# Prompt attention with the branch factors applied after the value products: rows of factors through DRAM, plain transposes, GpSimd adding the branches

## The chip, the cores and the metric

The kernel runs on one core of one Trainium2 chip. The metric is the device time of one execution in microseconds (us), lower is better. TensorE (PE), VectorE (DVE), ScalarE (ACT), GpSimd (POOL) and SyncE (SP, which here only issues DMAs) run side by side and meet at semaphores; each engine takes its own instructions in order.

## What is computed

One step of a decoder layer: half-step FFN, a mixer (sparse attention and a pooling mixer), a second FFN, a final norm. The change touches only the attention of the prompt (1024 tokens, 8 query heads of width 64 in 2 KV groups of 4). Each head has three branches over different keys, and their results are added with a gate:

```python
def masked_softmax(s, mask):
    s = jnp.where(mask, s, NEG_INF)
    m = jnp.max(s, axis=-1, keepdims=True)
    e = jnp.where(mask, jnp.exp(s - m), 0.0)
    return e / jnp.maximum(jnp.sum(e, axis=-1, keepdims=True), 1e-30)
...
    o = gates[..., 0:1] * o_c + gates[..., 1:2] * o_s + gates[..., 2:3] * o_w
```

With 16 selected blocks of 64 for 1024 prompt tokens, the selected branch is causal attention over all keys. For a query token and head the result is therefore the sum over the branches of a factor, gate / sum(e), times sum over the keys of e * v. The factor belongs to the query; it can be multiplied in before or after the product with v.

## The kernel before

The kernel is a row of stages with a barrier between them: compression of the cache, FFN 1, input projection, pooling, compression of the prompt, **prompt attention** (stage_attend_prompt, about 1618 to 2098 us), sample attention, output projection, FFN 2, finish.

Prompt attention runs a loop over the two KV groups g. In it, 128 query tokens at a time make a block qt = 0 to 7, and one more iteration, qt = 8, drains. Iteration qt has four **rows** r, one for each head: the scores of block qt and head r (selected keys into slc_bank, window keys and compressed blocks into win_bank; L1895 to L1932), maxima on VectorE (L1853 to L1859), exponentials with their sums on ScalarE (L1757 to L1765) into probs. Between them each row carries a quarter of the **value units** of the block before, qt - 1: one unit is 128 keys of one branch (64 for the compressed one), so block qt - 1 has qt selected units, up to five of the window and one compressed, 3 in the first block and 14 in the last; 74 for each g. For each unit

- TensorE **turns** the probabilities of the four heads (L1884): a matmul with probs as weights and a diagonal matrix that holds the factor of each token, so the factor is multiplied in while the tile is transposed;
- ScalarE takes the high half (L1733) and VectorE the low half (L1798) out of the turn bank, of which there are two;
- TensorE multiplies both halves by the values (L1948, L1949). The product of a unit is issued after the turn of the next one. All branches of a block are summed in one PSUM bank, out_bank[qt % 2].

In row 2 the query tile of the next block is turned first (L1890, a plain transpose of at_dup against the identity). The order is by hand: in each row TensorE issues selected scores, window scores, then its turns and products; VectorE the maxima, then the low halves; ScalarE the first high half, the selected exponential, the second high half, the window exponentials, the rest.

The factors come from VectorE (factors, L1813 to L1821), for heads 0 and 1 at the end of row 2 and for heads 2 and 3 at the end of row 3; GpSimd spreads each pair to diagonals (L1700), and the first turn of the next iteration waits for the second pair (L1882, wait on diag_ready). When a block is summed, ScalarE copies its upper half (L1738, the values' low halves) and VectorE adds it to the lower half in four pieces into mixT (take, L1830), in row 1 of the next iteration but one. SyncE issues nothing in this stage.

## Time and profile before

| what | us |
|---|---|
| median of 3 runs | 3283.76 (3279.31 to 3285.95) |
| the profiled execution | 3281.28 |
| its span | 3279.6 |
| prompt attention, within the span | about 480 |
| PE busy in the whole span | 2924.5 (89%) |
| DVE, ACT, POOL busy in the whole span | 1448.3, 905.5, 311.1 |

### The profile page before, as it was taken

The numbers are of one execution on the slowest core, as the hardware profiler recorded it, in microseconds if no ns is written. First come the engines' busy times: TensorE is split into PE (matmuls) and PEld (weight loads), VectorE is DVE, ScalarE is ACT, GpSimd is POOL, SyncE is SP. The second block draws the span as 40 slices with busy tenths as digits, with TensorE's granted clock in tenths as the row PEclk, the third lists the DMA queues.
The fourth block names the chain that finished last, engine by engine and source line by source line (L and its number), as shares of the span: only waits on it lengthen the run. The fifth ranks groups of instructions, "written<-read, shape, count | busy, mean of one in ns | idle before, by whom it ended". The sixth has DMA issues, their size and how long they took to land. (4 is left out here: it accounts for less than half of the span.)

```text
span 3279.6 us, 48743 instructions
## 1 busy us (share of the span) xinstructions
PE 2924.5 (89%) x18374; PEld 2688.3 (82%) x18374; DVE 1448.3 (44%) x2808; ACT 905.5 (28%) x1537; POOL 311.1 (9%) x294
## 2 busy tenths in 40 slices
PE   4999989999999997885789789687799999999997
PEld 4889879999999996884667667433589999999996
DVE  4444455544444445013255456312326454444445
ACT  4665651111111102111245345233222111111112
POOL 3444410000000001000011011211000000000000
PEclk9999999999999998997579879888899999999999
DMA  4212133211111102102100000365322111111101
GB/s 158 110 56 110 62 105 105 64 38 38 40 50 42 47 0 87 33 26 77 35 1 1 2 1 1 125 183 158 112 58 62 42 53 49 38 38 51 38 13 53
DMA packets 168574, 193.84 MB, mean 59 GB/s; under 512 B 11431, under 2 KB 154536, under 8 KB 165679
## 3 DMA queue, kind: packets, MB, share of 16 engines
q1 hardware_dynamic: 161623, 141.58, 14.2%
q0 software_dynamic: 6816, 50.49, 4.2%
q8 instruction: 81, 1.33, 0.2%
q14 instruction: 54, 0.44, 0.0%
HBM read 178.30 MB, written 17.91 MB: 60 GB/s over the span
## 5 line engine op out<-in xcount | busy, mean ns | idle before, releaser
L407 ACT ACTIVATE f_act_gate<-f_act_gate 128x352 f32<-128x352 f32 x132 | 65.8, 498 | 1186.2 <-DVE f_act_gate L464 1186.1
L501 DVE SCALAR_TENSOR_TENSOR trunk<-f_down,trunk 128x352 f32<-128x352 f32 x528 | 275.8, 524 | 207.8 <-PE f_down L104 207.8
L102 PE MATMUL f_up<-f_h_hi,f_gu_hi 128*128 128x352 f32 x1056 | 344.6, 326 | 0.0
L102 PE MATMUL f_gate<-f_h_hi,f_gu_hi 128*128 128x352 f32 x1056 | 344.3, 326 | 0.0
L104 PE MATMUL f_up<-f_h_hi,f_gu_lo 128*128 128x352 f32 x1056 | 342.8, 325 | 0.0
L104 PE MATMUL f_gate<-f_h_hi,f_gu_lo 128*128 128x352 f32 x1056 | 342.5, 324 | 0.0
L102 PE MATMUL f_down<-f_a_hi,f_wd_hi 128*128 128x352 f32 x1056 | 340.6, 323 | 0.0
L103 PE MATMUL f_gate<-f_h_lo,f_gu_hi 128*128 128x352 f32 x1056 | 340.5, 322 | 0.0
L103 PE MATMUL f_up<-f_h_lo,f_gu_hi 128*128 128x352 f32 x1056 | 340.1, 322 | 0.0
L103 PE MATMUL f_down<-f_a_lo,f_wd_hi 128*128 128x352 f32 x1056 | 338.5, 321 | 0.0
L104 PE MATMUL f_down<-f_a_hi,f_wd_lo 128*128 128x352 f32 x1056 | 338.1, 320 | 0.0
L102 PE MATMUL cs_sum<-cs_x_hi,cs_w_hi 128*128 128x256 f32 (+1 forms) x768 | 229.9, 299 | 32.6 <-DVE cs_x_lo L1152 21.4
L104 PE MATMUL cs_sum<-cs_x_hi,cs_w_lo 128*128 128x256 f32 (+1 forms) x768 | 217.5, 283 | 0.0
L103 PE MATMUL cs_sum<-cs_x_lo,cs_w_hi 128*128 128x256 f32 (+1 forms) x768 | 217.4, 283 | 0.0
L102 PEld LDWEIGHTS f_gate<-f_h_hi,f_gu_hi 128*128 128x128 f32 x1056 | 199.6, 189 | 1.3 <-DVE f_gu_lo L447 1.1
L102 PEld LDWEIGHTS f_up<-f_h_hi,f_gu_hi 128*128 128x128 f32 x1056 | 199.9, 189 | 0.0
L1884 PE MATMUL at_turn_bank<-at_diag,at_probs 128*128 128x128 f32 (+1 forms) x1184 | 177.7, 298 | 24.6 <-POOL at_diag L1700 20.3
L1884 PEld LDWEIGHTS at_turn_bank<-at_diag,at_probs 128*128 128x128 f32 (+1 forms) x1184 | 162.4, 203 | 45.3 <-issue 39.6
L103 PEld LDWEIGHTS f_gate<-f_h_lo,f_gu_hi 128*128 128x128 f32 x1056 | 198.8, 188 | 0.2
L103 PEld LDWEIGHTS f_up<-f_h_lo,f_gu_hi 128*128 128x128 f32 x1056 | 198.9, 188 | 0.0
L103 PEld LDWEIGHTS f_down<-f_a_lo,f_wd_hi 128*128 128x128 f32 x1056 | 198.4, 188 | 0.0
L102 PEld LDWEIGHTS f_down<-f_a_hi,f_wd_hi 128*128 128x128 f32 x1056 | 198.1, 188 | 0.0
(333 smaller groups left out, 5812.3 us busy)
## 6 DMA issues: line engine op xcount, KB each, us to landing
as_pages<-in_cache_kv_slc_dram SPq DMA_DIRECT2D x192, 128.0 KB, 2.3
f_gu_raw<-in_w_ffn_gate_dram SPq DMA_DIRECT2D x44, 512.0 KB, 4.5
f_gu_raw<-in_w_ffn_up_dram SPq DMA_DIRECT2D x44, 512.0 KB, 5.7
f_wd_raw<-in_w_ffn_down_dram SPq DMA_DIRECT2D x22, 1024.0 KB, 5.0
as_pages<-in_cache_kv_slc_dram POOLq DMA_DIRECT2D x64, 128.0 KB, 3.2
in_w_raw<-in_w_in_dram SPq DMA_DIRECT2D x4, 1304.0 KB, 5.9
x_saved<-trunk SPq DMA_DIRECT2D x1, 4224.0 KB, 16.2
trunk<-x_saved SPq DMA_DIRECT2D x1, 4224.0 KB
```

The source lines that it names most:

```text
L102: pe.matmul(out, w_hi, x_hi, start=first, stop=False)
L103: pe.matmul(out, w_hi, x_lo, start=False, stop=False)
L104: return pe.matmul(out, w_lo, x_hi, start=False, stop=last)
L407: act.activation(act_gate[:, b, :], act_gate[:, b, :], ACT.Silu).then_inc(silu_done, 1)
L501: dve.scalar_tensor_tensor(xT[:, m, chunk(c)], down_bank[n % 4][:, 0:CH], 0.5, xT[:, m, chunk(c)], ALU.mult, ALU.add).then_inc(down_free, 1)
L1884: tr = pe.matmul(bank[0:rows, h * P:(h + 1) * P], probs[qt % 2][:, h, lo:lo + rows], diag[:, qt % 2, h, branch, :], start=True, stop=True)
```

## The change

- The turn of a value unit is a transpose against the identity (L1909 of the new kernel) of the unscaled exponentials; it waits for the exponentials of all four heads instead of the diagonals. The diagonals and their GpSimd work are gone.
- Each of the three branches of a block is summed alone. The branches (selected, window, compressed) take the two out banks in turn. VectorE multiplies each closed sum by rows of factors (scale, L1858), 128 x 512 from PSUM and SBUF to SBUF, right after the low half of the unit that follows the branch's last; the compressed branch's comes behind the first unit of the next block.
- The factors of all four heads are made at once, at the end of row 0 of the next iteration (L1841 to L1849). SyncE writes them to DRAM transposed, 128 x 12 single floats, waits for that to land, and reads the 12 x 128 rows back into every partition (spread). Every scale of that block waits for spread.
- GpSimd adds the three scaled branches, copies the upper half and adds the halves (gather, four kinds of step), two iterations later, between its query copies; after the last iteration of g for the last two blocks. ScalarE's copy and VectorE's take are gone. GpSimd's program is no longer a loop over g, and it copies the first two key tiles of g = 1 ahead of the last two gathers of g = 0.

The core of the diff:

```diff
+    BRANCHES = (SLC, WIN, CMP)
+    ends = [[max(u for u, unit in enumerate(value_units(qt)) if unit[0] == branch) for branch in BRANCHES]
+            for qt in range(QT)]
+    behind = {}
+    for x, n in products.items():
+        _, qt, u = x
+        if u in ends[qt] and n + 1 < PRODUCTS:
+            follower = [y for y in products if products[y] == n + 1][0]
+            behind[follower] = (qt, ends[qt].index(u), BRANCHES[ends[qt].index(u)])
...
-        diag = mem.sb(scope, "at_diag", [P, 2, GROUP, 3, P])
+        spread = mem.sb(scope, "at_spread", [P, 3 * GROUP, P])
+        scaled = [mem.sb(scope, f"at_scaled{i}", [P, 3, GROUP, P]) for i in range(2)]
...
+            @block.sync
+            def _(sp):
+                for g in range(N_KV):
+                    for qt in range(QT):
+                        n = QT * g + qt
+                        sp.wait_ge(factor_ready, n + 1)
+                        if n >= 2:
+                            sp.wait_ge(spread_landed, 16 * (n - 1))
+                        sp.dma_start(factor_rows[qt % 2].rearrange("k p -> p k"),
+                                     factor[:, qt % 2].rearrange("p r b -> p (r b)"),
+                                     allow_slow_non_contiguous=True).then_inc(rows_saved, 16)
+                        sp.wait_ge(rows_saved, 16 * (n + 1))
+                        if n >= 1:
+                            sp.wait_ge(scaled_done, 3 * n + RING)
+                        sp.dma_start(spread[:], factor_rows[qt % 2].unsqueeze(0).to_broadcast([P, 3 * GROUP, P])
+                                     ).then_inc(spread_landed, 16)
...
+                def gather(g, qt):
+                    n, m = QT * g + qt, scaled[qt % 2]
+                    pool.wait_ge(scaled_done, 3 * n + 2 + RING)
+                    pool.tensor_tensor(m[:, 0], m[:, 0], m[:, 1], ALU.add).then_inc(added, 1)
+                    pool.wait_ge(scaled_done, 3 * n + 3 + RING)
+                    pool.wait_ge(added, 4 * n + 1)
+                    pool.tensor_tensor(m[:, 0], m[:, 0], m[:, 2], ALU.add).then_inc(added, 1)
+                    pool.wait_ge(added, 4 * n + 2)
+                    pool.tensor_copy(upper[:], m[HD:2 * HD, 0]).then_inc(added, 1)
+                    pool.wait_ge(added, 4 * n + 3)
+                    for half, sem in enumerate((added, out_taken)):
+                        pool.tensor_tensor(mixT[half * HD:(half + 1) * HD, 2 * g:2 * g + 2, qt * P:(qt + 1) * P],
+                                           m[0:HD, 0, half::2, :], upper[:, half::2, :], ALU.add).then_inc(sem, 1)
+                        if half == 0:
+                            pool.wait_ge(added, 4 * n + 4)
+                    pool.wait_ge(out_taken, n + 1 + RING)
...
+                        if qt >= 2:
+                            gather(g, qt - 2)
+                    if g + 1 < N_KV:
+                        for x in LEAD[:2]:
+                            duplicate(g + 1, x)
+                    for qt in range(QT - 2, QT):
+                        gather(g, qt)
...
-                                take_upper(g, qt - 2)
...
+                def factors(g, qt):
                     for i in range(2):
-                        dve.wait_ge(exped[i], HEADS * g + GROUP * qt + PAIR * (pair + 1) + ONE)
-                    if qt >= 2:
-                        dve.wait_ge(diag_ready, 2 * QT * g + 2 * (qt - 2) + pair + 1 + ONE)
-                    else:
-                        dve.wait_ge(diag_ready, 2 * QT * g + ONE)
-                    heads = slice(PAIR * pair, PAIR * pair + PAIR)
-                    f = factor[:, qt % 2, heads, :]
-                    s0 = STEPS * g + (4 * qt + 2 * pair + 2 if qt else 3 * pair)
-                    dve.tensor_scalar(f, sums[:, qt % 2, heads, :], 1e-30, None, ALU.max).then_inc(dve_step, 1)
+                        dve.wait_ge(exped[i], HEADS * g + GROUP * (qt + 1) + ONE)
+                    f = factor[:, qt % 2]
+                    s0 = STEPS * g + (2 * qt + 1 if qt else 0)
...
+                def scale(g, qt, n, branch):
+                    dve.wait_ge(pv_done, PRODUCTS * g + products[("v", qt, ends[qt][n])] + 1 + RING)
+                    dve.wait_ge(spread_landed, 16 * (QT * g + qt + 1))
+                    dve.wait_ge(out_taken, QT * g + qt - 1 + RING)
+                    rows = spread[:].rearrange("p (r b) n -> p b r n", b=3)[:, branch]
+                    dve.tensor_tensor(scaled[qt % 2][:, n], out_bank[(3 * qt + n) % 2][:].rearrange("p (r n) -> p r n", r=GROUP),
+                                      rows, ALU.mult).then_inc(scaled_done, 1)
...
+                                    if x[0] == "v" and x in behind:
+                                        scale(g, *behind[x])
+                            if qt > 0 and r == 0:
+                                factors(g, qt - 1)
+                    scale(g, QT - 1, 2, CMP)
...
-                            pe.wait_ge(diag_ready, 2 * QT * g + 2 * (qt + 1) + ONE)
+                        pe.wait_ge(exped[0 if branch == SLC else 1], HEADS * g + GROUP * (qt + 1) + ONE)
                         pe.nop(nofuse=True)
                         for h in range(GROUP):
-                            tr = pe.matmul(bank[0:rows, h * P:(h + 1) * P], probs[qt % 2][:, h, lo:lo + rows],
-                                           diag[:, qt % 2, h, branch, :], start=True, stop=True)
+                            tr = pe.transpose(bank[0:rows, h * P:(h + 1) * P], probs[qt % 2][:, h, lo:lo + rows],
+                                              K["ident"][:])
...
+                    n = BRANCHES.index(branch)
+                    first, last = u == (ends[qt][n - 1] + 1 if n else 0), u == ends[qt][n]
+                    bank = out_bank[(3 * qt + n) % 2]
                     pe.wait_ge(split, TURNS * g + at[x] + 1 + RING)
                     if v == 0:
                         pe.wait_ge(v_ready, g + 1)
-                    if u == 0:
-                        pe.wait_ge(out_taken, QT * g + max(0, qt - 1) + ONE)
+                    if first:
+                        pe.wait_ge(scaled_done, 3 * (QT * g + qt) + n + 1)
                     pe.nop(nofuse=True)
                     values = (vc_split[0:rows] if source is None else v_split[:, source[0], source[1]]
                               ).rearrange("p c d -> p (c d)")
-                    last = u == len(value_units(qt)) - 1
-                    pe.matmul(out_bank[qt % 2][:], values, turned_hi[v % 2][0:rows, :], start=(u == 0), stop=False)
-                    pe.matmul(out_bank[qt % 2][:], values, turned_lo[v % 2][0:rows, :], start=False,
+                    pe.matmul(bank[:], values, turned_hi[v % 2][0:rows, :], start=first, stop=False)
+                    pe.matmul(bank[:], values, turned_lo[v % 2][0:rows, :], start=False,
                               stop=last).then_inc(pv_done, 1)
-                    if last:
-                        pe.wait_ge(pv_done, PRODUCTS * g + v + 1 + RING)
-                        pe.nop().then_inc(out_done, 1)
```

TensorE at the end of row 2 of iteration 1, and behind the line of dots its row 3 (the scores between are left out). Before:

```order
L1876 REGISTER_ALU
L1884 MATMUL at_turn_bank_290<-at_diag,at_probs_277 128x128 x4
L1941 REGISTER_ALU
L1943 ISA
L1948 MATMUL at_out_bank_292<-at_turned_hi_283,at_v_split 128x512
L1949 MATMUL at_out_bank_292<-at_turned_lo_285,at_v_split 128x512
...
L1884 MATMUL at_turn_bank_291<-at_diag,at_probs_277 64x128 x4
L1939 REGISTER_ALU
L1948 MATMUL at_out_bank_292<-at_turned_hi_284,at_v_split 128x512
```

The same place after:

```order
L1902 REGISTER_ALU
L1909 MATMUL at_turn_bank_292<-ident,at_probs_277 128x128 x4
L1969 REGISTER_ALU
L1971 ISA
L1975 MATMUL at_out_bank_294<-at_turned_hi_285,at_v_split 128x512
L1976 MATMUL at_out_bank_294<-at_turned_lo_287,at_v_split 128x512
...
L1909 MATMUL at_turn_bank_293<-ident,at_probs_277 64x128 x4
L1967 REGISTER_ALU
L1971 REGISTER_ALU
L1975 MATMUL at_out_bank_295<-at_turned_hi_286,at_v_split 128x512
```

The instructions stand in the same places; the turn reads the identity, and the next branch's product goes to the other bank (295).

VectorE from the window maxima of row 0 of iteration 3 on. Before, the row's low half, then in row 1 the take of block 1:

```order
L1857 TENSOR_REDUCE at_neg_max<-at_win_bank 128x1
L1859 TENSOR_REDUCE at_neg_max<-at_win_bank 128x1
L1787 REGISTER_ALU
L1798 TENSOR_TENSOR at_turned_lo_285<-at_turn_bank_290,at_turned_hi_283 128x512
L1826 REGISTER_ALU
L1830 ISA
L1830 TENSOR_TENSOR trunk<-at_out_bank_293,at_upper 64x128
```

After, behind the same low half, the scale of block 1's compressed branch and the factors of block 2:

```order
L1881 TENSOR_REDUCE at_neg_max<-at_win_bank 128x1
L1883 TENSOR_REDUCE at_neg_max<-at_win_bank 128x1
L1820 REGISTER_ALU
L1831 TENSOR_TENSOR at_turned_lo_287<-at_turn_bank_292,at_turned_hi_285 128x512
L1854 REGISTER_ALU
L1858 TENSOR_TENSOR at_scaled_281<-at_out_bank_295,at_spread 128x512
L1841 TENSOR_SCALAR at_factor<-at_sums 128x12
...
L1843 RECIPROCAL at_factor<-at_factor 128x12
...
L1849 TENSOR_TENSOR at_factor<-at_factor,z 128x12
```

In row 2 of that iteration the first scale with these factors (block 2, selected branch) stands between two low halves:

```order
L1826 SCALAR_TENSOR_TENSOR at_q_split<-at_turn_bank_293,at_q_split 64x512
L1820 REGISTER_ALU
L1831 TENSOR_TENSOR at_turned_lo_288<-at_turn_bank_292,at_turned_hi_286 128x512
L1854 REGISTER_ALU
L1855 ISA
L1858 TENSOR_TENSOR at_scaled_280<-at_out_bank_294,at_spread 128x512
L1820 REGISTER_ALU
L1831 TENSOR_TENSOR at_turned_lo_287<-at_turn_bank_293,at_turned_hi_285 128x512
```

What moved on VectorE: the factors came from the ends of rows 2 and 3 to the end of row 0 of the next iteration, and the take became three scales.

## Rows read from the trace of the kernel before

**Rows 1.** Stretches of prompt attention: us, busy (x instructions) by engine, granted clock, DMA share.
```profile
1640.00:1656.00 16.00, 12.50 (x57) 11.16 (x58) 7.03 (x23) 6.95 (x29) 3.49 (x3) 0.52 0.00 1
...
1750.00:1775.00 25.00, 22.84 (x154) 18.44 (x153) 15.46 (x32) 12.08 (x29) 3.49 (x3) 1.00 0.00 1
...
sum 481.00, PE 398.98 PEld 321.53 DVE 250.63 ACT 220.94 POOL 60.87; mean PE 24.94 PEld 20.10 DVE 15.66 ACT 13.81 POOL 3.80
```

**Rows 2.** Groups of prompt attention: busy, mean ns of one, then idle before.
```profile
L1884 PE MATMUL at_turn_bank<-at_diag,at_probs 128*128 128x128 f32 (+1 forms) x1184 | 177.7, 298 | 24.6 <-POOL at_diag L1700 20.3 <-PE at_out_bank L1949 2.1 <-DVE at_turned_lo L1798 1.0
...
L1700 POOL TENSOR_TENSOR at_diag<-ident,at_factor 128x768 f32<-128x768 f32 x32 | 47.0, 1469 | 346.5 <-DVE at_factor L1821 346.5
...
L1830 DVE TENSOR_TENSOR trunk<-at_out_bank,at_upper 64x128 f32 x64 | 18.1, 283 | 15.0 <-ACT at_upper L1738 14.1
...
L1815 DVE RECIPROCAL at_factor<-at_factor 128x6 f32<-128x6 f32 x32 | 6.1, 191 | 1.1
```

**Rows 3.** Waits of prompt attention: us in total, times, longest.
```profile
PE at_turn_bank L1884 <- POOL at_diag L1700: 20.3, 14, 3.1
...
DVE trunk L1830 <- ACT at_upper L1738: 14.1, 10, 1.7
```

**Rows 4.** One row without a query turn (qt 6, r 1): start, duration, instruction.
```profile
1773.85 0.99 PEld L1884 LDWEIGHTS at_turn_bank<-at_diag,at_probs 128*128 128x128 f32 x8
...
1775.14 0.60 ACT L1733 ACTIVATE at_turned_hi<-at_turn_bank 128x512 fp32r<-128x512 f32 x1 [2.50 <-PE at_turn_bank L1884]
...
1775.63 1.00 ACT L1757 ACTIVATE at_probs<-at_slc_bank,at_neg_max 128x896 f32<-128x896 f32 x1
...
1777.25 0.69 DVE L1798 TENSOR_TENSOR at_turned_lo<-at_turn_bank,at_turned_hi 128x512 fp32r<-128x512 f32 x1 [0.71 <-ACT at_turned_hi L1733]
...
1778.39 0.19 PEld L1895 LDWEIGHTS at_slc_bank<-at_kT_hi,at_q_split 128*128 128x128 f32 x1
```

**Rows 5.** The next row, with a query turn (r 2), timeline.
```profile
1780.60 0.43 PEld L1890 LDWEIGHTS at_turn_bank<-ident,at_dup 128*128 128x128 f32 x4
...
1780.99 0.97 PEld L1884 LDWEIGHTS at_turn_bank<-at_diag,at_probs 128*128 128x128 f32 x8
...
1781.30 0.60 ACT L1728 ACTIVATE at_q_split<-at_turn_bank 128x512 fp32r<-128x512 f32 x1 [2.31 <-PE at_turn_bank L1890]
```

**Rows 6.** VectorE's low halves that frame the later scale, timeline, two iterations.
```profile
1688.30 0.69 DVE L1798 TENSOR_TENSOR at_turned_lo<-at_turn_bank,at_turned_hi 128x512 fp32r<-128x512 f32 x1 [2.85 <-ACT at_turned_hi L1733]
...
1700.03 0.69 DVE L1798 TENSOR_TENSOR at_turned_lo<-at_turn_bank,at_turned_hi 128x512 fp32r<-128x512 f32 x1 [0.46 <-ACT at_turned_hi L1733]
...
1772.05 0.69 DVE L1798 TENSOR_TENSOR at_turned_lo<-at_turn_bank,at_turned_hi 128x512 fp32r<-128x512 f32 x1 [0.86 <-ACT at_turned_hi L1733]
...
1783.40 0.69 DVE L1798 TENSOR_TENSOR at_turned_lo<-at_turn_bank,at_turned_hi 128x512 fp32r<-128x512 f32 x1 [0.78 <-ACT at_turned_hi L1733]
```

**Rows 7.** VectorE's low halves in the last block's drain, timeline.
```profile
2076.72 0.69 DVE L1798 TENSOR_TENSOR at_turned_lo<-at_turn_bank,at_turned_hi 128x512 fp32r<-128x512 f32 x1 [1.35 <-ACT at_turned_hi L1733]
...
2086.36 0.69 DVE L1798 TENSOR_TENSOR at_turned_lo<-at_turn_bank,at_turned_hi 128x512 fp32r<-128x512 f32 x1 [0.67 <-ACT at_turned_hi L1733]
...
2089.54 0.69 DVE L1798 TENSOR_TENSOR at_turned_lo<-at_turn_bank,at_turned_hi 128x512 fp32r<-128x512 f32 x1 [0.67 <-ACT at_turned_hi L1733]
```

**Rows 8.** DMA issues: KB each, median us to landing.
```profile
as_pages<-in_cache_kv_slc_dram SPq DMA_DIRECT2D x192, 128.0 KB, 2.3
...
f_gu_raw<-in_w_ffn_gate_dram SPq DMA_DIRECT2D x44, 512.0 KB, 4.5
...
as_kc<-kc_saved SPq DMA_DIRECT2D x1, 1024.0 KB, 4.9
```

**Rows 9.** GpSimd's groups in the whole kernel: a two-operand step of nearly 512 columns.
```profile
L1009 POOL TENSOR_TENSOR cs_x_lo<-cs_x,cs_x_hi 128x516 fp32r<-128x516 f32 x128 | 170.1, 1329 | 231.2 <-ACT cs_x_hi L1066 231.2
```

**Rows 10.** The last stage, where TensorE only transposes: instructions of fin_bank, granted clock.
```profile
3271.00:3272.00 1.00, 1.00 (x7) 1.00 (x6) 0.61 (x2) 0.50 0.00 0
...
3274.00:3275.00 1.00, 1.00 (x12) 0.92 (x10) 1.00 (x3) 1.00 0.70 283
```

More of the change, by code:

```diff
@@ L1599, in stage_attend_prompt @@
     HEADS = QT * GROUP
-    PAIR = 2
     def win_tiles(qt):
@@ L1675, in _ @@
             @block.gpsimd
             def _(pool):
-                pool.sem_inc(diag_ready, ONE)
                 def duplicate(g, x):
                     m = dups[x]
-                    before = TURNS * g + ONE
-                    if m >= 2:
-                        before += at[[y for y in dups if dups[y] == m - 2][0]] + 1
+                    before = ONE
+                    if DUPS * g + m >= 2:
+                        earlier = [y for y in dups if dups[y] == (m - 2) % DUPS][0]
+                        before += TURNS * ((DUPS * g + m - 2) // DUPS) + at[earlier] + 1
@@ L1705, in _ @@
-                with pool.Fori(0, N_KV) as g:
-                    for x in LEAD:
-                        duplicate(g, x)
+                def gather(g, qt):
[14 more added lines that the diff above has]
+                    pool.wait_ge(out_taken, n + 1 + RING)
@@ L1708, in _ @@
+                for x in LEAD:
+                    duplicate(0, x)
+                for g in range(N_KV):
+                    if g > 0:
+                        for x in LEAD[2:]:
+                            duplicate(g, x)
                     for qt in range(QT):
@@ L1710, in _ @@
                             duplicate(g, ("q", qt + 1))
-                        for pair in range(2):
-                            diagonals(g, qt, pair)
+                        if qt >= 2:
[5 more added lines that the diff above has]
+                        gather(g, qt)
             @block.scalar
@@ L1820, in factors @@
                         dve.wait_ge(dve_step, s0 + 3)
-                    dve.tensor_tensor(f, f, z[:, qt, bass.ds(OFF_GATE + g * 3 * GROUP + 3 * PAIR * pair, 3 * PAIR)]
+                    dve.tensor_tensor(f, f, z[:, qt, bass.ds(OFF_GATE + g * 3 * GROUP, 3 * GROUP)]
                                       .rearrange("p (r b) -> p r b", b=3), ALU.mult).then_inc(factor_ready, 1)
-                def take(g, t):
-                    dve.wait_ge(upper_done, QT * g + t + 1)
-                    for r in range(GROUP):
-                        half = slice((r % 2) * HD, (r % 2 + 1) * HD)
-                        cols = slice(r * P, (r + 1) * P)
-                        last = dve.tensor_tensor(mixT[half, bass.ds(2 * g + r // 2, 1), t * P:(t + 1) * P],
-                                                 out_bank[t % 2][0:HD, cols].unsqueeze(1), upper[:, cols].unsqueeze(1),
-                                                 ALU.add)
-                    last.then_inc(out_taken, 1)
+                def scale(g, qt, n, branch):
[5 more added lines that the diff above has]
+                                      rows, ALU.mult).then_inc(scaled_done, 1)
                 with dve.Fori(0, N_KV) as g:
@@ L1845, in _ @@
                         for r in range(GROUP):
-                            if r == 1 and qt >= 2:
-                                take(g, qt - 2)
                             n = GROUP * qt + r
@@ L1862, in _ @@
                                     low(g, x)
-                            if qt < QT and r >= 2:
-                                factors(g, qt, r - 2)
-                    take(g, QT - 1)
+                                    if x[0] == "v" and x in behind:
[3 more added lines that the diff above has]
+                    scale(g, QT - 1, 2, CMP)
             @block.tensor
```

46 lines of the change are left out of this document (16 added, 30 removed).

## The prediction

> **What bounds the kernel now.** I read the stretches first, since the change touches one stage only. Prompt attention is 481 us of the span, and TensorE is busy in 399 of them, VectorE in 251, ScalarE in 221, GpSimd in 61 [rows 1]. In the middle of the stage TensorE works 22.8 of 25 us at the full granted clock; at the start of a group it works 12.5 of 16 at a clock of 0.52 [rows 1]. The costliest group is the turn, 1184 matmuls or eight for each of 148 units, 177.7 us busy [rows 2]. Then the waits: TensorE waited 20.3 us for the diagonals, in 14 of 16 blocks, and VectorE 14.1 us for ScalarE's copy of the upper half [rows 3].
>
> A busy TensorE isn't yet the bound, so I followed one row in order of time [rows 4]. The row starts its first turn at 1773.85; the first high half starts at 1775.14, the selected exponential behind it at 1775.63, the second low half at 1777.25, and the next row's scores at 1778.39. The scores of a head wait for the exponentials of the head before and stand behind the second product, so a row is a ring: scores, first turn, ScalarE's first high half and exponential, second high half, second low half, product, scores. The first turn is on the ring; the second and third are beside ScalarE's work. The reader is to see this, since it decides what a cheaper turn is worth: once a row, not three times.
>
> **The turn, removed and added.** The turn of a unit with diagonals takes 1.29 us from its first weight load to ScalarE's start (1773.85 to 1775.14) [rows 4]. The query tile is already a plain transpose of the same four 128 x 128 tiles, four records instead of eight: 0.70 us (1780.60 to 1781.30), and TensorE goes on after 0.39 us (1780.99) [rows 5]. So a plain turn on the ring saves 0.59 us. Rows of r = 2 start with the query turn, which doesn't change; their ring passes through it, and I give them nothing. That leaves rows 1 and 3 of iteration 1, rows 0, 1, 3 of iterations 2 to 6 and four rows of iteration 7: 21 for each g, 42 x 0.59 = 25 us. Were TensorE the bound throughout, it would be 148 x (0.99 - 0.39) = 89 us; were the low halves the bound, nothing. I take 25, since the ring is what the rows show.
>
> In the drain there are no scores. Two turn banks make two units a round: low halves at 2086.36 and 2089.54, 3.18 us for two units [rows 7], with one turn on the round. 14 rounds in the two groups, each 0.59 us shorter: 8 us. The most it could be is TensorE's own work, 2 x 0.60 a round, 17 us; the least nothing.
>
> **The wait for the diagonals** goes: 20.3 us, all of it ahead of the first turn, on the ring [rows 3]. What is late next there is the exponentials of the fourth head, for which the scores wait anyway. GpSimd's 32 diagonals, 1.47 us each, go with it [rows 2].
>
> **VectorE's own work.** Removed for each block: four adds of 0.28 us [rows 2], about 0.9 us of waiting (14.1 / 16) [rows 3] and one of two sets of factors. Added: three scales, 128 x 512 from PSUM, which I price as the low half of that shape, 0.69 us [rows 4]: 2.1 us against some 2.0 and the factors. I put them at nothing together; VectorE is busy in half the stage, and ScalarE loses its copy, which was beside the ring. Were none covered, 48 x 0.69 = 33 us would be lost, less 32 regained; so 0 with a bound of 10 either way. Two out banks now turn over three times a block: a product that opens a branch waits for the scale two branches back, which is a whole row old except where that scale itself is late.
>
> **The factors' way through DRAM** is the added wait, and it decides the case. SyncE has nothing else in its queue. The chain: factors done, write of 1536 single floats, its landing, read of 128 x 6 KB = 768 KB, its landing, then the scale of the selected branch. Queued behind that scale on VectorE are all later low halves and maxima, so TensorE and ScalarE stop soon after.
>
> How much room there is, from the low halves that stand there now. In iteration 6 the last low half of row 0 ends at 1772.74 and the first unit's of row 2 at 1784.09 [rows 6], 11.35 us apart; the factors take 0.75 of it (three small steps, the reciprocal 0.19 us [rows 2], with a semaphore between them; an estimate from that row), and the row between shortens by 0.59: 10.0 us of room. In iteration 3 it is 1688.99 to 1700.72 [rows 6], 11.7 us, but the take (1.1), the compressed scale (0.7), the factors (0.75) and the turns of two rows come off: 8.5. In the drain the low half of the third unit ends at 2077.41, that of the ninth at 2087.05 [rows 7], 9.6 us; six units at 0.3 less each and the factors off: 6.9. I take 8.5 for iterations 1 to 4, 10 for 5 to 7 and 6.9 for the drain.
>
> How long the way is. No row shows a write of single floats. The nearest is the load of 1024 pieces of 512 bytes: 4.5 us, against 2.3 for 128 pieces of 1 KB, so 2.2 us for about 900 more pieces [rows 8]; 1536 pieces make 2.3 + 3.5 = 5.8 us. From below it is 2.3 us, as a small DMA; from above I take twice the time of a piece, since a piece smaller than anything in the trace may need its surroundings read and written: 2.3 + 7 = 9.3. The read lies between 512 KB in 4.5 and 1024 KB in 4.9 us [rows 8], fewer and larger pieces: 4.2. From below 3.6, half way from the small load to the large one; from above 6, a quarter over the 1024 KB, since all partitions read the same 6 KB and no row does that. With 0.3 for the semaphores the way takes 10.3 us, between 6.2 and 15.6. Per group the stall is 4 x 1.8 + 3 x 0.3 + 3.4 = 11.5, or **23 us** in all; at 6.2 none; at 15.6 it is 4 x 7.1 + 3 x 5.6 + 8.7 = 53.9, or 108 us. I take 23, by the row of small pieces.
>
> The Trainium skill speaks against this write: DMA: Bandwidth & Descriptors, Rules for kernel authors, has a strided last dimension lower to one descriptor for each element, and its section Bandwidth measured about 10.5 ns a packet, which with its fixed 2.0 us would make the write an estimated 3.0 us. The sum would then lose its stalls almost whole and end near 3237. No trace here shows it.
>
> **The tail.** The stage now ends after scale 0.69, GpSimd's second add, copy, and two half adds. A GpSimd add of two operands over 516 columns takes 1.33 us [rows 9]: 0.69 + 1.33 + 0.66 + 1.33 = 4.0 us, against copy 0.60 and 4 x 0.28 = 1.7. Plus 2.3 us, once; in g = 0 it lies beside the engines' own turn of the loop. In the iterations the gather, 5.3 us, has a whole iteration of over 15 us.
>
> **The clock.** TensorE gets less to do, and at the start of each group it runs at 0.52 while busy 78% [rows 1]. I allow 5 us for a rise that comes later. The row that bears on it: in the last stage TensorE does nothing but transposes, and its clock stands at 0.50 at 3271 and at 1.00 at 3274 [rows 10]. TensorE: Matmul & The Clock Gate of the Trainium skill, Part 4: PE-mode transpose, says that transposes don't count as busy for the clock in the same way; the trace disagrees, and by it I don't lower the clock of the whole stage.
>
> **The sum.** 25 + 8 + 20.3 = 53 off; 23 + 2.3 + 5 = 30 on; net 23 off the profiled 3281.3: 3258. The median stands 2.5 above that execution, so **3261**.
>
> **The rivals.** *The way is hidden.* If it lands within 7 us, no block waits, and the time is 3283.8 - 53 + 7 = 3238. For it: the queue is empty and the DMA engines are idle in this stage (share 0.00 [rows 1]). Against it: two landings one after the other, each 2.3 at the very least. *The way is long: slower.* Each further us costs 16, eight blocks in two groups. The gain is used up at 12 us: 2 x (4 x 3.5 + 3 x 2 + 5.1) = 50 against 53 - 7 = 46. At 14 us it is 2 x (4 x 5.5 + 3 x 4 + 7.1) = 82: 3320; at 15.6, 3346. It takes only that a float costs 70 ns more in its queue than I reckon, and nothing in the trace excludes that. *A tie,* where the way takes 11.5 to 12.2 us. *The clock halves.* If transposes don't hold it, the lower level, 1.2 GHz, stays. TensorE took 12.5 / 57 = 0.22 us for each instruction at a clock of 0.52 and 22.8 / 154 = 0.15 at 1.00 [rows 1], 1.48 times. Of its 399 us, 310 are left without the 89; three quarters of them, at full clock now, would grow by 0.48 x 232 = 111 us, nearly all on the ring: 3367. Against it stand the transposes alone, which raised the clock [rows 10].
>
> **How the numbers follow.** Forecast (way 7.5 to 11.5 us) 0.37, 3240 to 3275; hidden 0.2; tie 0.08; long way 0.3; clock 0.05. A measurement of this kernel can tell about 0.2%, 6.6 us. With the edges of the cases, faster than 3277 has 0.58, same 0.1, slower than 3290 0.32. For 8 in 10 the range takes in the hidden way and most of the long one: 3234 to 3338.
>
> **What would show it.** The median from issue to landing of the two new DMAs, 5.8 and 4.2; VectorE's idle time ahead of the scales put down to spread, 23 us in 16; the turn with four records and no wait on GpSimd; rows of r = 1 some 0.6 us shorter and rows of r = 2 not; the drain's rounds 2.6 us. Wrong would be the sum if rows shorten by three turns (then TensorE was the bound), if the write lands in over 8 us, or if the granted clock of the middle of the stage leaves 1.00.

## The result and the profile after

| | us |
|---|---|
| before, median of 4 runs | 3284.57 (3279.31 to 3285.95) |
| after, median of 4 runs | 3326.59 (3323.61 to 3329.84) |
| ratio | 1.0131, 95% interval 1.0114 to 1.0149 |
| predicted | 3261 (3234 to 3338) |

The change costs 42 us. The time lies in the range; the direction was wrong. All of it is in prompt attention, which now ends about 2139 instead of 2098.

Stretches of the kernel after, columns as in [rows 1]:

```profile
1640.00:1656.00 16.00, 12.45 (x63) 10.76 (x63) 6.48 (x19) 6.74 (x27) 0.00 (x0) 0.58 0.04 0
1656.00:1676.00 20.00, 12.11 (x45) 8.13 (x44) 9.22 (x20) 5.95 (x21) 5.21 (x6) 0.60 0.15 40
...
1750.00:1775.00 25.00, 16.67 (x94) 12.53 (x94) 13.43 (x23) 10.13 (x26) 3.96 (x5) 0.86 0.14 33
...
sum 521.00, PE 345.95 PEld 253.73 DVE 262.21 ACT 209.81 POOL 88.23; mean PE 23.06 PEld 16.92 DVE 17.48 ACT 13.99 POOL 5.88
```

TensorE has 53 us less to do than in [rows 1] (345.95 for 398.98) and the stage takes 40 us more. In the middle it works 16.67 of 25 us where it worked 22.84, and the granted clock is 0.86 there instead of 1.00.

Groups, the first two answering to [rows 2], the turn and the scale:

```profile
L1909 PE MATMUL at_turn_bank<-ident,at_probs 128*128 128x128 f32 (+1 forms) x592 | 104.9, 306 | 4.8 <-DVE at_q_split L1826 4.8
...
L1858 DVE TENSOR_TENSOR at_scaled<-at_out_bank,at_spread 128x512 f32<-128x512 f32 x48 | 32.8, 683 | 108.2 <-DMA at_spread<-factor_rows 106.1 <-PE at_out_bank L1976 2.1
```

The eight records of a turn are four, the wait for GpSimd of [rows 3] is gone, and in its place the scales wait 106.1 us for the factor rows. The view of the waits:

```profile
PE at_out_bank L1975 <- DVE at_turned_lo L1831: 116.1, 73, 8.8
DVE at_scaled L1858 <- DMA at_spread<-factor_rows: 106.1, 16, 8.7
```

All 16 blocks wait, 6.6 us each on average, and TensorE's products wait 116.1 us in all for low halves, the longest of them for those that stand behind a waiting scale on VectorE. One block in order of time, SyncE's two issues, then VectorE:

```profile
1785.63 0.37 SPq L1693 DMA_DIRECT2D factor_rows<-at_factor  x1
1797.09 0.32 SPq L1699 DMA_DIRECT2D at_spread<-factor_rows  x1
```

```profile
1785.21 0.39 DVE L1849 TENSOR_TENSOR at_factor<-at_factor,z 128x12 f32<-128x12 f32 x1
...
1794.56 0.69 DVE L1831 TENSOR_TENSOR at_turned_lo<-at_turn_bank,at_turned_hi 128x512 fp32r<-128x512 f32 x1 [0.78 <-ACT at_turned_hi L1773]
1800.91 0.69 DVE L1858 TENSOR_TENSOR at_scaled<-at_out_bank,at_spread 128x512 f32<-128x512 f32 x1 [5.66 <-DMA at_spread<-factor_rows]
```

The write takes 11.46 us from its issue to the read's (1785.63 to 1797.09). The read lands in 4.2, as the view of the DMA issues has it:

```profile
at_spread<-factor_rows SPq DMA_DIRECT2D x16, 768.0 KB, 4.2
```

I had put the write at 5.8 and its upper bound at 9.3. The 16 blocks lie between 9.5 and 12.1, with a mean of 11.1.

### The profile page after: what moved, and what is told of

It reads as the page before. It is cut to its first block and busy times, and to the rows that moved or that the text cites. A ratio compares the mean times of both kernels' runs of the same rounds, so it can differ in the third digit from the quotient of the medians.

```text
span 3321.9 us, 47407 instructions
## 1 busy us (share of the span) xinstructions
PE 2872.5 (86%) x17782; PEld 2619.5 (79%) x17782; DVE 1459.9 (44%) x2742; ACT 894.8 (27%) x1521; POOL 338.8 (10%) x342
## 5 line engine op out<-in xcount | busy, mean ns | idle before, releaser
L104 PEld LDWEIGHTS f_down<-f_a_hi,f_wd_lo 128*128 128x128 f32 x1056 | 197.9, 187 | 0.0
L104 PEld LDWEIGHTS f_gate<-f_h_hi,f_gu_lo 128*128 128x128 f32 x1056 | 197.9, 187 | 0.0
```

The lines of the kernel that those rows point to most:

```text
L104: return pe.matmul(out, w_lo, x_hi, start=False, stop=last)
```

## The experiments

All times are medians; the kernel before stood at 3282.6, 3282.0 and 3280.6 beside the three groups of runs (first the four from no_way to pe_rows, then b_ident, b_no_factors and pe_win, then flat, b_plain and b_fill), so sums across groups are good to about 2 us.

| kernel | us | against before, 95% |
|---|---|---|
| no_way | 3201.4 | 0.9740 to 0.9773 |
| turn_mm | 3239.3 | 0.9847 to 0.9880 |
| half_write | 3300.9 | 1.0044 to 1.0078 |
| pe_rows | 3209.7 | 0.9762 to 0.9794 |
| b_ident | 3240.6 | 0.9856 to 0.9894 |
| b_no_factors | 3238.3 | 0.9851 to 0.9885 |
| pe_win | 3223.0 | 0.9800 to 0.9835 |
| flat | 3202.7 | 0.9754 to 0.9781 |
| b_plain | 3206.3 | 0.9754 to 0.9784 |
| b_fill | 3266.8 | 0.9948 to 0.9974 |

**no_way: what is the way worth?**

```diff
-            @block.sync
-            def _(sp):
...
+                pool.memset(spread[:], 1.0).then_inc(spread_landed, 16)
...
-                    dve.wait_ge(spread_landed, 16 * (QT * g + qt + 1))
+                    dve.wait_ge(spread_landed, 16)
```

> The kernel after without the factors' way: SyncE does nothing, GpSimd sets spread to 1.0 once, no scale waits for a DMA (leaves out the factors, all other work stays). Theory (the wait of 106 us ahead of the scales is the whole loss, and it lies on the ring): that wait gone, 3326.6 - 93 = 3234 (93 is what the rows r = 2 and the two drains are longer for it), near the hidden-way rival of the prediction, 3238; granted clock of the middle of the stage back at 1.00. Rival A (the stall also covered work: three scales a block and GpSimd's adds cost something of their own): 3255 to 3275. Rival B (transposes alone don't hold the clock): 3280 or more, with a clock under 0.9 in the middle of the stage.

3201.4, lower than every case. The way costs 125 us (123 with each kernel set against the kernel before of its own group), not the expected 93, and the rest of the change gains 81, not the prediction's 46. None of the cases on record had these sizes. A table of the rows shows where; each number is the time from one row's selected exponential to the next one's (g = 0):

| iteration | kernel | into row 1 | row 2 | row 3 | next row 0 |
|---|---|---|---|---|---|
| 2 | before | 5.73 | 4.69 | 4.87 | 7.37 |
| 2 | after | 4.77 | 4.69 | 9.88 | 6.54 |
| 2 | no_way | 3.65 | 3.58 | 4.14 | 4.24 |
| 6 | before | 7.36 | 6.17 | 8.33 | 8.16 |
| 6 | after | 6.27 | 6.17 | 15.28 | 6.37 |
| 6 | no_way | 6.27 | 6.17 | 7.82 | 6.36 |

The stall stands in the interval into row 3 (7.5 us in iteration 6). In iteration 2 after is also 1.1 us slower into rows 1 and 2, where nothing waits for a DMA. The stretches show the clock there; after, then no_way:

```profile
1656.00:1660.00 4.00, 0.50 (x3) 0.05 (x1) 0.00 (x0) 0.59 (x1) 0.00 (x0) 1.00 0.34 107
1660.00:1664.00 4.00, 0.45 (x1) 0.47 (x2) 2.21 (x6) 1.15 (x6) 0.00 (x0) 0.51 0.24 94
1664.00:1668.00 4.00, 4.00 (x15) 2.39 (x14) 2.06 (x5) 1.15 (x5) 1.28 (x1) 0.50 0.00 0
1668.00:1672.00 4.00, 3.73 (x16) 2.90 (x15) 3.29 (x8) 1.25 (x7) 2.76 (x4) 0.50 0.13 1
```

```profile
1656.00:1676.00 20.00, 15.15 (x91) 10.05 (x88) 14.96 (x31) 11.30 (x38) 6.50 (x7) 1.00 0.00 0
```

TensorE is nearly idle from 1656 to 1664 in after; the clock goes from 1.00 to 0.50 (1.2 GHz) and stays there while the next rows run. In no_way it has the same kind of work and stays at 1.00. Over the stage, after is 82 us longer than no_way in the intervals into row 3, 21 in the two drains, and 21 in the 48 other intervals, which hold no stall. All of these last 21 lie in iterations 1 to 4; in iterations 5 to 7 the same intervals agree within 0.1 us. So the intervals with the 106 us of stall are 103 longer, and the rows behind them 21. The lower clock is shown beside the latter in iteration 2; that it makes up all 21 is inferred.

**turn_mm: what is the plain turn worth?** On no_way's base:

```diff
-                            tr = pe.transpose(bank[0:rows, h * P:(h + 1) * P], probs[qt % 2][:, h, lo:lo + rows],
-                                              K["ident"][:])
+                            tr = pe.matmul(bank[0:rows, h * P:(h + 1) * P], probs[qt % 2][:, h, lo:lo + rows],
+                                           K["ident"][:], start=True, stop=True)
```

> As no_way, but each turn is an ordinary matmul against the identity, as it was before in form, not a transpose (eight records for four; nothing waits for it more than before). Theory of the prediction (a turn counts once a row, on the ring): 42 x 0.59 in the rows and 14 x 0.59 in the drains, 33 us over no_way. Rival A (TensorE is the bound): 148 x 0.60 = 89 us over no_way. Rival B (the low halves on VectorE are the bound): within 7 us of no_way.

38 us over no_way, beside the expected 33 and far from 89. In iteration 6 the intervals are 7.03, 6.19, 8.32 and 7.08 for no_way's 6.27, 6.17, 7.82 and 6.36: no_way is shorter into rows 1, 3 and 0 and the same into row 2, whose first turn is the query's. Of the 38 us, 32 lie in the rows and 6 in the drains. So a turn counts once a row, as the prediction's ring has it, and not three times.

**half_write: is it the number of floats?**

```diff
-                        sp.dma_start(factor_rows[qt % 2].rearrange("k p -> p k"),
-                                     factor[:, qt % 2].rearrange("p r b -> p (r b)"),
+                        k = 3 * GROUP if n < 2 else 3 * GROUP // 2
+                        sp.dma_start(factor_rows[qt % 2][0:k].rearrange("k p -> p k"),
+                                     factor[:, qt % 2].rearrange("p r b -> p (r b)")[:, 0:k],
```

> The kernel after, but from the third block on only 6 of the 12 factor rows are written (768 single floats for 1536), the read stays whole (leaves out half of the factors). Theory (the write costs by the piece): 2.3 + half of (11.5 - 2.3) = 6.9 us from issue to the read's issue, the way 11.3 instead of 15.8, stalls about 40 us instead of 106, time about 3265. Rival (a fixed price of the transposed form, or the landing of 128 partitions): write stays above 10 us, time within 7 us of 3326.

Missed by both. The writes of six rows took 8.2 to 10.6 us, 9.1 on average, not 6.9 and mostly not above 10; the stalls were 82 us, and the time fell by 26 instead of 60. Half of the pieces save about 2 of 11 us, so most of the write isn't paid by the piece.

**pe_rows: a write of whole rows.** TensorE transposes the 128 x 12 factors in one more step of the turn banks:

```diff
-                        sp.dma_start(factor_rows[qt % 2].rearrange("k p -> p k"),
...
+                        sp.dma_start(factor_rows[qt % 2], rows_sb[:, qt % 2]).then_inc(rows_saved, 16)
...
+                        tr = pe.transpose(bank[0:3 * GROUP, 0:P], factor[:, x[1] % 2].rearrange("p r b -> p (r b)"),
+                                          K["ident"][:])
...
+                        act.activation(rows_sb[:, x[1] % 2], bank[0:3 * GROUP, 0:P], ACT.Copy).then_inc(hi_done, 1)
```

> The kernel after, but TensorE transposes the factors (128 x 12 to 12 x 128, one more step of the turn banks in row 1, ScalarE copies it out), and SyncE writes 12 rows of 512 bytes instead of 1536 single floats; same result. Theory: write 2.3 us, read 4.2, and about 2 us more until the rows stand in SBUF: the way 8.8 us instead of 15.8, stalls under 10 us in all; the extra step costs up to 1 us a block on the ring: 3238 + 6 + 10 = 3254, faster than both kernels. Rival (the read or its landing is what takes the time, not the write): 3300 or more. Rival (the extra step in the ring of turn banks costs as much as it saves): 3280.

3209.7, faster than both kernels. The write of 12 x 512 bytes takes 1.29 us from issue to issue. The extra step costs 1.2 us in the interval into row 2 (iteration 6: 7.38 for 6.17). No scale waits for spread. The expectation was 44 us too high: it started from 3238 without stalls, where no_way measured 3201.

**b_ident and b_no_factors: where do the other 43 us come from?** On the kernel before:

```diff
-                            diagonals(g, qt, pair)
...
-                            pe.wait_ge(diag_ready, 2 * QT * g + 2 * (qt + 1) + ONE)
+                        pe.wait_ge(exped[0 if branch == SLC else 1], HEADS * g + GROUP * (qt + 1) + ONE)
...
-                                           diag[:, qt % 2, h, branch, :], start=True, stop=True)
+                                           K["ident"][:], start=True, stop=True)
```

b_no_factors also drops the call of factors in rows 2 and 3.

> The kernel before with the turn's matmul against the identity (eight records a turn as before), waiting for the exponentials; the diagonals and their GpSimd work are gone, the factors are still made on VectorE at the ends of rows 2 and 3, the take stays (leaves out the multiplication by the factors). It removes the wait for the diagonals alone. Theory (that wait is worth what the waits say, 20.3 us, as the prediction had it): 3283 - 20 = 3263. Rival A (it is worth all that turn_mm gained over the kernel before, 43 us): 3240. Rival B (the exponentials are late next): over 3275.

> As b_ident, and VectorE makes no factors in the rows at all (leaves out the factors). Theory (the factors at the end of row 3 wait for ScalarE's last exponentials and stand ahead of the next row's maxima; the rows r = 3 are 19 us shorter in turn_mm than in the kernel before, which the prediction put at nothing): 20 us below b_ident, 3243. Rival (the rest of the gain is in the take and ScalarE's copy, or in GpSimd's order between the groups): within 6 us of b_ident.

b_ident came out at 3240.6: taking out a wait of 20.3 us [rows 3] was worth 41. Between the two profiled executions, 19 us lie in the intervals into row 0, 13 in the other rows and 11 in the drains. The theory that the wait is worth its length falls. b_no_factors lies within b_ident's runs, so the factors on VectorE cost nothing there. I had read the shorter intervals into row 0 as the factors' place; they were the diagonals. What doubled the wait shows in the kernel before at the turn from iteration 3 to 4:

```profile
1700.00:1704.00 4.00, 3.98 (x29) 3.13 (x27) 2.92 (x7) 1.56 (x5) 0.94 (x1) 1.00 0.03 6
...
1708.00:1712.00 4.00, 2.87 (x16) 2.32 (x15) 1.55 (x3) 0.56 (x2) 2.02 (x2) 0.76 0.00 0
1712.00:1716.00 4.00, 3.61 (x14) 2.87 (x13) 1.03 (x2) 1.79 (x5) 0.00 (x0) 0.50 0.00 0
1716.00:1720.00 4.00, 4.00 (x29) 3.54 (x28) 2.82 (x7) 2.02 (x7) 0.00 (x0) 0.89 0.00 0
```

Behind the wait the clock is at 0.50, and 14 matmuls are done from 1712 to 1716 for 29 in each of the slices 1700 and 1716. The front's stretches of 16 to 25 us average this away. Iteration 4's first row, which runs there, takes 7.82 us into row 1, for b_ident's 6.31. To test the clock:

**b_fill: the wait kept, but filled.** On the kernel before, whole:

```diff
                         if u == 0:
+                            pe.nop(nofuse=True)
+                            for h in range(5):
+                                pe.matmul(bank[:, (h % 4) * P:(h % 4 + 1) * P], K["ident"][:], K["ident"][:],
+                                          start=True, stop=True)
                             pe.wait_ge(diag_ready, 2 * QT * g + 2 * (qt + 1) + ONE)
```

> The kernel before, whole, with five matmuls of the identity (128 x 128 each, some 1.2 us together) issued ahead of the wait for the diagonals in the first turn of each block; their output is overwritten. The wait for the diagonals thereby isn't shorter, TensorE is only busy in it. Theory (b_ident gained 42 us for a wait of 20.3 because TensorE's granted clock falls to its lower level behind the wait and stays there for 4 us and more): the clock no longer falls, and a good part of the other 22 us comes back although work is added: 3262 to 3272. Rival (the 22 us come from the rows' order or from GpSimd, not from the clock): 3282 or more.

3266.8: useless work (the five matmuls took 1.36 us where I looked, at 1704.69) makes the kernel 13.7 us faster. The same stretches of time now, and one in the drain of g = 0:

```profile
1708.00:1712.00 4.00, 3.19 (x21) 2.65 (x22) 1.50 (x3) 2.86 (x8) 0.00 (x0) 1.00 0.00 0
1712.00:1716.00 4.00, 3.40 (x27) 3.06 (x26) 3.64 (x9) 2.48 (x5) 0.00 (x0) 1.00 0.00 0
...
1824.00:1828.00 4.00, 3.70 (x13) 2.91 (x13) 0.69 (x1) 0.97 (x2) 0.00 (x0) 0.50 0.02 4
```

So some 14 of the 21 us beyond the wait are the clock. Most of them came back in rows 1 and 2 of iterations 2 to 4 (iteration 2: 4.15 and 3.57 us, for 5.73 and 4.69 before). In iterations 5 and 6 b_fill's intervals are those of the kernel before within 0.05 us, and there the kernel before keeps its clock behind waits of 1.2 and 1.0 us (1.00 from 1735 to 1747 and from 1764 to 1776). A wait of 1.1 us ahead of iteration 4 had brought it down, so the length of the wait alone doesn't tell. In the drains the clock fell all the same and nothing came back; what the 11 us that b_ident saved there are made of, beyond the wait, stays open.

**b_plain: the sum closed.** b_ident with pe.transpose for pe.matmul in the turn.

> b_ident with plain transposes for the turns: the kernel before, less the diagonals, and with the new turn, but with neither factors' way nor scales nor GpSimd's adds (leaves out the factors). Theory (the turn is worth 38 us here too, as turn_mm against no_way): 3241 - 38 = 3203, so scales, adds and tail cost nothing beside no_way's 3201. Rival (VectorE's scales cost something that other parts of the change give back): 3190.

3206.3: the turn is worth 34 us here. The scales, GpSimd's adds and the tail, which b_plain lacks and no_way has, cost nothing that can be seen; b_plain is even 5 us slower. Two things stand beside that. Its clock was 0.53 in 1656 to 1676 for no_way's 1.00, in g = 0 alone; pe_rows had such a late rise in g = 1 alone (1.00 from 1656 to 1676, but 0.50 from 1858 to 1868), so it can differ between two groups of one execution, and why stays open. And in both groups b_plain is 0.45 to 0.63 us slower into row 1 of iterations 3 to 5, the interval in which its VectorE still has the take.

**write_curve and write_shape: what makes the write dear?** Another size or shape in each block of one kernel, each kernel run once; the first two lines are write_curve's. apart is a DRAM tensor of 128 rows of 1024 bytes, close one of 128 rows of 64 bytes.

```diff
+                            sp.dma_start(out[0:k].rearrange("k p -> p k"), f[:, 0:k],
...
+                            sp.dma_start(out.rearrange("k p -> (k p)").rearrange("(p k) -> p k", k=3 * GROUP),
...
+                            sp.dma_start(apart[:, 0, 0:1], f[:, 0:1],
...
+                            sp.dma_start(close[:, 0:1], f[:, 0:1],
...
+                            sp.dma_start(close.rearrange("p k -> (p k)")[0:P * k].rearrange("(p k) -> p k", k=k), f[:, 0:k],
```

> The kernel after with a write of another size in each block: 12, 12, 8, 6, 4, 3, 2, 1 factor rows for the blocks of g = 0, then for g = 1 all twelve untransposed as 128 pieces of 48 bytes, 12, 10, 6, 4, 2, 1, and 128 pieces again (leaves out or misplaces factors). From SyncE's issue of the write to its issue of the read. Known: 11.5 us for 12 rows, 8.5 for 6, and 1.3 for 12 pieces of 512 bytes. Theory A (a fixed part and a price per piece, 3.9 ns, from the two known sizes): 5.5 + 0.5 per row, so 6.0 us for one row, and the 128 pieces of 48 bytes as one row of 128 singles, 6.0. Theory B (pieces to neighbouring words of DRAM hold each other up, which saturates): one row 3 us or less and a curve that flattens; the 128 pieces of 48 bytes under 3 us.

> The kernel after with a write of another shape in each block of a group: blocks 0 and 1 as it is (1536 single floats); block 2 one factor row, 128 single floats to neighbouring words of DRAM; 3 the same 128 floats, each 1024 bytes from the next; 4 each 64 bytes from the next; 5, 6, 7: 128 pieces of 8, 16 and 32 bytes to neighbouring places (leaves out or misplaces factors). From SyncE's issue of the write to its issue of the read. Theory A (a piece of 4 bytes is dear of itself): 7 us in blocks 2, 3 and 4, and less from 8 bytes on. Theory B (pieces that share a short stretch of DRAM hold each other up): 7 us in block 2, under 2 us in block 3, and growing less with the size of the piece. Theory C (the form of the source, one float from each of 128 partitions, costs it): 7 us in all.

By rows: 12 rows 9.8 to 10.9 us, 6 rows 8.2 and 9.8, 4 rows 8.1 and 10.1, 2 rows 7.9 and 9.4, 1 row 6.9 and 7.3; the whole factors as 128 pieces of 48 bytes 1.41, twice. Theory A had the flat curve and missed the 48 bytes; theory B had the 48 bytes and missed the single row, which it put at 3 us or less. In write_shape, SyncE's issues of write and read, in turn for one row of neighbouring floats, for floats 1024 bytes apart, and for pieces of 8 and of 16 bytes:

```profile
1696.88 0.32 SPq L1699 DMA_DIRECT2D factor_rows<-at_factor  x1
1703.63 0.32 SPq L1714 DMA_DIRECT2D at_spread<-factor_rows  x1
1719.51 0.32 SPq L1702 DMA_DIRECT2D factor_apart<-at_factor  x1
1720.91 0.32 SPq L1714 DMA_DIRECT2D at_spread<-factor_rows  x1
...
1767.72 0.32 SPq L1709 DMA_DIRECT2D factor_close<-at_factor  x1
1770.71 0.32 SPq L1714 DMA_DIRECT2D at_spread<-factor_rows  x1
1794.35 0.32 SPq L1709 DMA_DIRECT2D factor_close<-at_factor  x1
1795.76 0.32 SPq L1714 DMA_DIRECT2D at_spread<-factor_rows  x1
```

6.75, 1.40, 2.99 and 1.41 us; the second group gave 7.53, 2.35, 2.98 and 1.40. Floats 64 bytes apart took 3.16 and 1.41, and pieces of 32 bytes 1.40 twice. Of write_shape's theories B holds: the same 128 floats cost 1.4 to 2.4 us when 1024 bytes apart and about 7 side by side. A piece of 4 bytes isn't dear of itself, and neighbours aren't either from 16 bytes on; dear are pieces of 4 bytes, and less so of 8, side by side. Why, and why 12 rows cost 11 and not 7 us, no run shows. The Trainium skill, DMA: Bandwidth & Descriptors, Specifications, says that below 512 bytes a transfer does a read-modify-write; no run here shows one. Pieces of 48, 32 and 16 bytes landed in 1.4 us all the same, so to be that small isn't enough to make a write dear here.

**flat: the way without a transpose.** The factors are written as they stand, and the scale reads them with a step of 12 floats:

```diff
-                        sp.dma_start(factor_rows[qt % 2].rearrange("k p -> p k"),
+                        sp.dma_start(factor_rows[qt % 2].rearrange("k p -> (k p)").rearrange("(p k) -> p k", k=3 * GROUP),
...
-                    rows = spread[:].rearrange("p (r b) n -> p b r n", b=3)[:, branch]
+                    rows = (spread[:].rearrange("p k n -> p (k n)")
+                            .rearrange("p (n r b) -> p b r n", b=3, r=GROUP)[:, branch])
```

> The kernel after, but nothing is transposed on the way: SyncE writes the factors as they stand, 128 pieces of 48 bytes, reads them back into every partition in that order, and each scale reads spread with a step of 12 floats; same result. Theory (the write costs 1.4 us in this form, as in write_curve; the way is 1.4 + 4.2 = 5.6 us and shorter than the room; nothing is added elsewhere): no_way's 3201, within 4. Rival A (VectorE reads a stride of 48 bytes more slowly, say 1.4 us for 0.68 a scale, 48 of them, partly on the ring): 3215 to 3240. Rival B (the room isn't there while other things are late): 3210 to 3220 with a wait for spread of over 5 us.

3202.7 (3202.1 to 3206.5), 2.3% faster than before and 1.4 us above no_way's median (3.4 with each set against its own kernel before). Its DMA issue of the write, and the group of its scales:

```profile
factor_rows<-at_factor SPq DMA_DIRECT2D x16, 6.0 KB, 1.4
```

```profile
L1858 DVE TENSOR_TENSOR at_scaled<-at_out_bank,at_spread 128x512 f32<-128x512 f32 x48 | 50.6, 1054 | 0.0
```

No scale waits; from issue to issue the writes took 1.40 to 2.57 us. Rival A's premise is true, a scale takes 1.05 us for 0.68, 48 of them 18 us in all; its price isn't: no interval of iteration 6 is over 0.3 us longer than in no_way. So the factors' way costs nearly nothing in this form, and what made the change slow is the form of the write.

**pe_win: pe_rows without the extra step.** The factors are made in the middle of row 0, behind its first low half, and transposed into spare columns of the window bank in row 1.

```diff
+                                    if r == 0 and qt > 0 and x == turns(qt, r)[0]:
+                                        factors(g, qt - 1)
...
+                                        pe.wait_ge(exped[1], HEADS * g + GROUP * qt + r + ONE)
+                                        turn_rows(g, qt - 1)
```

> As pe_rows (12 rows of 512 bytes written), but the extra step isn't in the ring of turn banks: the factors are made behind the first low half of row 0, TensorE transposes them into spare columns of the window bank ahead of row 1's window scores, VectorE copies them out ahead of the window maximum; same result as the reference's. Theory (the extra step costs pe_rows 1.2 us in each row r = 1 of iterations 5 to 7 and a little in the first three iterations of g = 1, and nothing waits for the way): 3210 - 7 = 3203, no_way's 3201 within 3. Rival (VectorE's steps in the middle of row 0 delay the low half and with it the row): 3210 or more.

The rival: 3223.0. Into row 2 of iteration 6 it is 6.17 as in no_way, but into row 1 it is 7.41 for 6.27: the three steps of the factors and their gaps took 1.46 us there (1776.34 to 1777.80), and they stand ahead of a low half; at the row's end, in no_way, they cost nothing seen. The lead isn't the whole of it: in iteration 2 the interval is 6.15 for 3.65, and the two drains, in which two scales waited 6.1 us in all for spread, contrary to the expectation, are 9 us longer.

## Why the prediction was wrong, step by step

Times in us. The terms are measured in different kernels and needn't add up to 42.

| term | predicted | measured | by |
|---|---|---|---|
| plain turns, rows and drains | -33 | -38, -34 | turn_mm, b_plain |
| wait for the diagonals | -20 | -41 | b_ident |
| VectorE's own work | 0 ± 10 | none seen (no_way 5 faster) | b_plain against no_way |
| clock from less work | +5 | none in no_way; a late rise in b_plain and pe_rows | stretches |
| the tail | +2.3 | about +2.8 | from the last low half, after and before |
| the way | +23 | +125 | after against no_way |

- **The step that failed** is the price of the write. I took 5.8 us "by the row of small pieces" and bounded it at 9.3; it took 11.1 on average. The row had 512-byte pieces and says nothing about words that share a stretch of DRAM. The bound was made by doubling the price of a piece, which keeps the wrong form: one row of 128 floats already costs 7 us. Nor did the lower bound hold that each landing takes 2.3 us at the very least: pe_rows' write took 1.29. The text's "70 ns more in its queue" is too much as well: 5.3 us too little over 1536 floats on 16 DMA engines is 55 ns a float on each. And the 3.0 us that it worked out from the Trainium skill, DMA: Bandwidth & Descriptors, Bandwidth, divides 10.5 ns a packet by 16 engines without saying so; one packet behind another it would be 18 us, and the measured 11.1 is neither.
- **The room and the rate were right.** From the end of the factors to the start of the scale the way took 15.6 us on average; less a stall of 6.6 that leaves 9.0 us of room, and the three values taken give 8.9. At 15.6 us the text has 108 us of stall; the trace has 106. The read was put at 4.2, and its median landing is 4.2. That the way met its own upper bound is luck: the write went 1.8 us over its bound of 9.3, and the read, 4.5 us from issue to scale, stayed 1.5 under its bound of 6.
- **The diagonals' wait** was taken at its length. This is the second failed step, in the other direction: it was worth twice that, for two thirds of the surplus because TensorE's clock fell behind it (b_fill). The text weighed the clock for the amount of work and not for the gaps. The same mechanism fits the 21 us that the rows behind the new stalls are longer. TensorE: Matmul & The Clock Gate of the Trainium skill, HAM oscillation, describes waits for a DMA between bursts that bring the lower level back each time; the rows of after agree (1.00 in the slice from 1656, then 0.51 and 0.50 in the next two, while TensorE does almost nothing from 1656 to 1664).
- **The turn** was right in mechanism and close in size: 32 us in the rows for the 25 worked out, 6 in the drains for 8. In the drain a round takes 2.72 us in no_way (low halves at 1801.71 and 1804.43) for 3.18 in [rows 7] and the predicted 2.6.
- **The tail** takes 4.7 us (last scale 2134.32, GpSimd's last add ends 2139.02) for the 4.0 worked out. From the last low half to the end it is 6.4 us after and 3.6 before.
- **The rival that came true** is the long way. It gave 3346 at 15.6 us; the rest of the gain, 81 instead of 46, brought the time down, and the slower rows behind the stalls took 20 of it back. That 3327 lies within the range is luck too: two steps failed in opposite directions, and without the underrated wait the time would have lain above 3338. The rival of the halved clock didn't come: with the same transposes no_way's clock is 1.00 from 1656 to 1676.

## What to carry to other kernels

A transposing write of single floats to DRAM was dear here because neighbouring words were written as pieces of their own: write in the order in which the partitions hold the data, and let the engine that reads it do the stride. A wait of TensorE can cost its length and the lower clock behind it, so read the granted clock in slices of a few us around each wait before pricing it. When a term is bounded from a row of another form, widen the bound by what the form could change and not by a factor on its price.

## What the hardware showed

- 128 floats from 128 partitions to one 512-byte stretch of DRAM: 6.75 to 7.5 us; the same 1024 bytes apart 1.4 and 2.35 (write_shape); 128 pieces of 48 bytes 1.41 in write_curve, 1.40 to 2.57 in flat; 12 pieces of 512 bytes 1.29 (pe_rows), all from issue to issue.
- Five useless matmuls a block ahead of a wait made the whole kernel 13.7 us faster (b_fill).
- A VectorE multiplication of 128 x 512 with one operand at a step of 12 floats took 1.05 us (flat), with a step of one 0.68 (after).
- A step over 128 x 12 elements on VectorE took 0.16 to 0.90 us; the runs don't tell why.
